# Low parts of eight mixed right sides at each layer border: GpSimd in place of VectorE

## The chip, the core and the metric

The kernel runs on one core of one Trainium2 chip. A core has five engines that run side by side and wait for each other by semaphores: TensorE (PE, matmuls; its weight loads are shown as PEld), VectorE (DVE), ScalarE (ACT), GpSimd (POOL), and SyncE (SP), which here only issues transfers. The metric is the device time of one execution in microseconds, lower is better.

## What is computed

Two transformer layers, one after the other, on a sequence of 1024 tokens with 1024 channels, all in float32:

```python
# first layer (one of depth 1), x: [1, 1024, 1024]
h = rmsnorm(x, norm1_g); proj = h @ w_in            # differential and forgetting attention
...
x = x + mix @ w_out
h2 = rmsnorm(x, norm2_g)
x = x + (silu(h2 @ w_gate) * (h2 @ w_up)) @ w_down
x = rmsnorm(x, normf_g)
# second layer
p = rmsnorm(x, g_attn_2) @ w_in_2                   # two convolutions, stick-breaking attention
...
x = x + concatenate([y_a, y_b, y_c]) @ w_out_2
h2 = rmsnorm(x, g_ffn_2)
x = x + square(relu(h2 @ w_ff1_2)) @ w_ff2_2
return rmsnorm(x, g_final_2)
```

In the kernel the norm's gain is applied ahead of the product and its root behind it, when the product leaves PSUM.

## The kernel before

**Products in three matmuls.** PE multiplies in a format that is shorter than float32. So each factor is a high part (a rounded copy, made by ScalarE) and a low part (the factor minus its high part). A product of one 128x128 block of weights with 128x512 columns is three matmuls: high by high (L1606), low weights by high (L1608), high weights by low (L1611). The low parts of the weights are made on GpSimd (L2408, `lows` or `late_r`, out of `values` or `late` and `wh`), their high parts on ScalarE (L2172). L1611 is the only one of the three that waits for the low part of the right side.

**Right sides.** They are the two big buffers R0 and R1, each with high and low parts of eight rows of 128x1024. The new input of a feed-forward part goes to R1: its row e is made when the output projection of the attention (`second_pass`) gives row e of X. VectorE adds up X (L1970, from PSUM), ScalarE rounds it to the high part (L2321) and VectorE makes the low part (L2026, 128x1024). PE mixes two works there: the last rows of the output projection and the first tiles of the next product (`dense_together`), which take row e of R1 as soon as it is there.

**The layer border.** So I call the stretch from the first L1970 to the first down product: 639 to about 720 us in the first layer, 1787 to about 1861 us in the second. (It lies between the attention and the feed-forward part of a layer.) The sum of the squares of X for the norm's root is taken there as well: ScalarE squares a row (L2331), GpSimd adds it to `mix` (L2467, 128x1024), PE sums over partitions (L1651), VectorE scales (L1821), ScalarE takes the root in two steps (L2215, L2219) and VectorE makes it exact (L1834 to L1838). With that root the first tiles leave PSUM (L2036, L2045 in the first layer, L2065 in the second), and their banks become free for other products.

**The mixed right sides.** Most feed-forward products are done in Strassen's way, seven products in place of eight (`dense_seven`; the products are called P1 to P7). Four of the seven take sums and differences of quarters of the input as their right side. They are made once at each border and kept in R0: for j = 0 to 3 and a = 0 to 3 the steps

- `right_z` (ScalarE, L2182), once for each j;
- `right_sum` (VectorE, L2002): X times gain, plus or minus another, 128x512, to R0f;
- `right_hi` (ScalarE, L2187): the high part;
- `right_lo` (VectorE, L2009): the low part, 128x512, sum minus high part.

P6, P5, P7 and P4 of the first group of seven read a = 1, 0, 2 and 3 in this order (the table `SEVEN_FIRST`, and `first_ready`, which says what each waits for). P7 and P4 are the last two; their eight low parts, a = 2 and a = 3, are the eight later ones.

**What sets the order.** Nobody writes it out. Each step says what it needs and gives; `engine_orders` lays the steps out by an estimate of their durations, gives each a due time from who needs it, and repeats that three times. It keeps the order among steps of one kind on one engine and chooses freely among kinds. So moving a step to another engine also moves its neighbours. PSUM has eight banks; a product waits until what stood in its bank has been taken out (`claim`, `next_bank`), for the down products by L2013, which adds PSUM to X.

## Time and profile before

| | us |
|---|---|
| three runs, median | 2492.11 |
| three runs, lowest and highest | 2489.48, 2495.3 |
| the profiled execution, device time | 2491.23 |
| its span in the profile | 2489.4 |
| busy in the span: PE, DVE, ACT, POOL | 2436.0, 1711.6, 1029.5, 1045.9 |

The span lies 1.8 us under the device time of the same execution. Times in the rows below count from the start of the span. A row of the timeline gives start and duration, the line of the kernel, the operation, what it writes and reads with shapes, how many neighbours of one kind are merged (x2), and in square brackets how long the engine had been idle before and who ended that. A record of DVE lasts until its last write; the next may start some 0.08 us before that.

### The profile page before, as it was taken

The page shows a single profiled execution, that of the slowest core. Times are in us where ns is not written, and L with a number is a line of the kernel's source. Part 1 is how long each engine was busy: PE and PEld are TensorE (multiplying, and loading weights), DVE is VectorE, ACT ScalarE, POOL GpSimd, SP SyncE. Part 2 cuts the span into 40 slices and gives each one's busy share as a digit, 9 for nine tenths or more (in the row PEclk, how much of TensorE's full clock was granted, in tenths as well). Part 3 has the DMA queues.
Part 4 walks back from the last instruction along what each step waited for, and adds up shares of the span by engine and source line. Part 5 has one row for each costly group of instructions (what it writes and reads, how often), then busy time and mean ns, then how long its engine had stood idle before and what let it go on. Part 6 is the DMA issues. An engine that isn't in the chain of part 4 may idle for free.

```text
span 2489.4 us, 31281 instructions
## 1 busy us (share of the span) xinstructions
PE 2436.0 (98%) x11654; PEld 1999.9 (80%) x11654; DVE 1711.6 (69%) x2373; ACT 1029.5 (41%) x1735; POOL 1045.9 (42%) x718
## 2 busy tenths in 40 slices
PE   9999999999899999999999999999989999999998
PEld 7776788888688888888887878887868888888886
DVE  6766757673786666666679866777497666666663
ACT  6455656552542322222246436554252232323233
POOL 4666552211534444444454553331343343434344
PEclk9999999999999999999999999999999999999998
DMA  4211221132111111111123852223211111112121
GB/s 162 76 56 47 86 60 44 54 116 76 39 47 53 55 55 56 51 51 51 55 59 111 188 127 68 60 76 105 66 39 56 47 56 47 57 46 60 43 64 72
DMA packets 156261, 170.20 MB, mean 68 GB/s; under 512 B 11088, under 2 KB 114256, under 8 KB 155984
## 3 DMA queue, kind: packets, MB, share of 16 engines
q1 hardware_dynamic: 152944, 156.67, 20.9%
q0 software_dynamic: 3168, 11.54, 2.5%
q8 instruction: 94, 1.54, 0.3%
q14 instruction: 55, 0.45, 0.1%
HBM read 122.55 MB, written 15.20 MB: 55 GB/s over the span
## 4 chain that ended last, share of the span: by engine, by line
PE 87%; DVE 6%; ACT 2%; issue 2%; POOL 1%; DMA 1%; SPq 0%; DVEq 0%; POOLq 0%; ACTq 0%
PE PS L1606 25%; PE PS L1611 25%; PE PS L1608 25%; PE PS L1702 3%; PE PS L1689 2%; PE PS L1723 2%; PE PS L1720 2%; PE PS L1683 2%; DVE R0f L2002 1%; DVE R L2026 1%; PE PS L1686 1%; DVE X L1970 1%; PE PS L1688 0%; DVE sm L1887 0%; PE PS L1670 0%
## 5 line engine op out<-in xcount | busy, mean ns | idle before, releaser
L1606 PE MATMUL PS<-R,wh 128*128 128x512 f32 x2952 | 1167.1, 395 | 3.9 <-DVE XP L1964 0.9
L1611 PE MATMUL PS<-R,wh 128*128 128x512 f32 x2952 | 1153.8, 391 | 14.3 <-DVE R L2026 14.1
L2408 POOL TENSOR_TENSOR lows<-values,wh 128x512 fp32r<-128x512 f32 (+1 forms) x410 | 596.0, 1456 | 1039.9 <-ACT wh L2172 931.8
L1608 PE MATMUL PS<-R,lows 128*128 128x512 f32 x2512 | 980.7, 390 | 1.6 <-POOL lows L2408 1.6
L1611 PEld LDWEIGHTS PS<-R,wh 128*128 128x128 f32 x2952 | 554.8, 188 | 137.6 <-DVE R L2026 19.2
L1606 PEld LDWEIGHTS PS<-R,wh 128*128 128x128 f32 x2952 | 555.7, 188 | 115.5 <-issue 4.1
L2172 ACT ACTIVATE wh<-values 128x512 fp32r<-128x512 f32 (+1 forms) x411 | 256.0, 623 | 721.4 <-PE PS L1611 685.0
L1608 PEld LDWEIGHTS PS<-R,lows 128*128 128x128 f32 x2512 | 472.7, 188 | 94.2 <-issue 4.1
L2013 DVE TENSOR_TENSOR X<-PS,X 128x512 f32<-128x512 f32 x400 | 272.2, 690 | 237.3 <-PE PS L1611 237.2
L2408 POOL TENSOR_TENSOR late_r<-late,wh 128x512 fp32r<-128x512 f32 x83 | 122.5, 1476 | 136.8 <-ACT wh L2172 97.5
L1608 PE MATMUL PS<-R,late_r 128*128 128x512 f32 x440 | 171.2, 389 | 0.0
L1990 DVE TENSOR_TENSOR stage<-PS,stage 128x512 f32<-128x512 f32 x154 | 104.5, 687 | 80.9 <-PE PS L1611 79.9
L2284 ACT ACTIVATE PT<-PS 128x512 fp32r<-128x512 f32 (+1 forms) x200 | 108.1, 552 | 101.2 <-PE PS L1702 94.0
L1689 PE MATMUL PS<-R 128*128 128x512 f32 (+2 forms) x288 | 116.8, 406 | 0.0
L1683 PE MATMUL PS<-R 128*128 128x512 f32 (+2 forms) x288 | 108.3, 376 | 6.5 <-ACT Pb L2267 4.0
L1887 DVE TENSOR_REDUCE sm<-PS 128x1 f32<-128x128 f32 (+7 forms) x128 | 95.5, 750 | 27.2 <-PE PS L1689 26.6
L1702 PE MATMUL PS<-ident,Pb 128*128 128x128 f32 x720 | 107.3, 274 | 5.1 <-DVE Pb L1899 3.2
L1911 DVE TENSOR_TENSOR_SCAN Pb<-TABF,vec 128x128 f32<-128x128 f32 (+3 forms) x64 | 97.1, 1521 | 17.5 <-ACT TABF L2276 9.1
L2172 ACT ACTIVATE wh<-late 128x512 fp32r<-128x512 f32 x83 | 52.3, 631 | 128.6 <-PE PS L1611 112.7
L1702 PEld LDWEIGHTS PS<-ident,Pb 128*128 128x128 f32 x720 | 85.9, 141 | 23.1 <-issue 6.4
L1934 DVE TENSOR_TENSOR PT<-PS,PT 128x512 fp32r<-128x512 f32 (+1 forms) x120 | 74.8, 631 | 33.4 <-ACT PT L2284 32.9
L1608 PEld LDWEIGHTS PS<-R,late_r 128*128 128x128 f32 x440 | 82.6, 188 | 17.1
(269 smaller groups left out, 2812.9 us busy)
## 6 DMA issues: line engine op xcount, KB each, us to landing
values<-w_in_dram SPq DMA_DIRECT2D x88, 256.0 KB, 2.9
values<-w_ff_dram SPq DMA_DIRECT2D x88, 256.0 KB, 2.8
R<-R SPq DMA_DIRECT2D x96, 128.0 KB, 2.3
X<-X POOLq DMA_DIRECT2D x22, 512.0 KB, 5.8
values<-w_up_dram SPq DMA_DIRECT2D x38, 256.0 KB, 3.0
values<-w_gate_dram SPq DMA_DIRECT2D x36, 256.0 KB, 2.9
late<-w_ff_dram SPq DMA_DIRECT2D x36, 256.0 KB, 2.9
values<-w_down_dram SPq DMA_DIRECT2D x32, 256.0 KB, 2.7
```

The source lines that it names most:

```text
L1606: e.matmul(PS[:, b, :], wh, high, start=s["start"], stop=False)
L1608: e.matmul(PS[:, b, :], wl, high, start=False, stop=False)
L1611: m = e.matmul(PS[:, b, :], wh, low, start=False, stop=s["stop"])
L1683: e.matmul(S2[:, k0:k1], q, u.KH[:, a, k0:k1], start=True, stop=False)
L1689: m = e.matmul(S2[:, k0:k1], q, u.KL[:, a, k0:k1], start=False, stop=True)
L1702: m = e.transpose(PS[:, s["tb"], at:at + 128], T.Pb[:, s["slot"], par, 128 * kt:128 * kt + 128], T.ident[:, :])
L1911: e.tensor_tensor_scan(dst[:, ::-1], bt[:, ::-1], T.zeros(n), 1.0, ALU.mult, ALU.add).then_inc(*sg.up("p", j["key"]))
L1990: e.tensor_tensor(stage[s["i"]], PS[:, s["b"], :], stage[s["k"]], ALU.add).then_inc(*sg.up("seven", s["key"]))
L2013: e.tensor_tensor(x, PS[:, s["b"], :], x, ALU.add).then_inc(*sg.up("x", s["key"]))
L2172: e.activation(T.wh[:, piece.h, 0:m], T.wv[piece.v][:, 0:m], ACT.Copy).then_inc(*sg.up("w_hi", piece.n))
L2284: e.activation(T.PT[:, s["x"], 0, 0:m], PS[:, s["tb"], 0:m], ACT.Copy, bias=bias).then_inc(*sg.up("pt_hi", key))
L2408: e.tensor_tensor(T.wl[piece.v][:, 0:m], T.wv[piece.v][:, 0:m], T.wh[:, piece.h, 0:m].bitcast(F), ALU.subtract).then_inc(*sg.up("w_lo", pi ...
```

## The change

The eight low parts with a = 2 and a = 3 are made by GpSimd, with the same subtraction, and counted on a semaphore of their own, `right_late_lo`. The products P7 and P4 of the first group wait for that one. Two waits of VectorE stay as they were for a = 0 and a = 1.

```diff
--- before.py
+++ after.py
@@ -1321,7 +1321,7 @@
 
     def first_ready(tag):
         rows = [[("post_hi", (tag, e)), ("post_lo", (tag, e))] for e in range(8)]
-        sums = [[[("right_hi", (tag, j, a)), ("right_lo", (tag, j, a))] for j in range(4)] for a in range(4)]
+        sums = [[[("right_hi", (tag, j, a)), ("right_lo" if a < 2 else "right_late_lo", (tag, j, a))] for j in range(4)] for a in range(4)]
         return dict(P1=rows[0::2], P2=rows[1::2], P3=rows[1::2], P5=sums[0], P6=sums[1], P7=sums[2], P4=sums[3])
 
     mix_ready = [[] for _ in range(8)]
@@ -2000,12 +2000,11 @@
             for before in {0: [], 1: [0], 2: [], 3: [0, 1, 2]}[a]:
                 w.wait_ge(*sg.at("right_sum", (tag, j, before)))
             e.scalar_tensor_tensor(out, x, g, other, ALU.mult, ALU.add if a == 1 else ALU.subtract).then_inc(*sg.up("right_sum", (tag, j, a)))
-        elif kind == "right_lo":
+        elif kind == "right_lo" and s["a"] < 2:
             j, a, tag = s["j"], s["a"], s["tag"]
             lo, hi = T.right(1, j, a), T.right(0, j, a)
             w.wait_ge(*sg.at("right_hi", (tag, j, a)))
-            if a < 2:
-                w.wait_ge(*sg.at("right_sum", (tag, j, (1, 3)[a])))
+            w.wait_ge(*sg.at("right_sum", (tag, j, (1, 3)[a])))
             e.tensor_tensor(lo, T.right_sum(j, a), hi.bitcast(F), ALU.subtract).then_inc(*sg.up("right_lo", (tag, j, a)))
         elif kind == "down_evac":
             x = T.XF[:, s["e"], cols(s["half"])]
@@ -2448,6 +2447,11 @@
             e.tensor_tensor(va, va, y, ALU.mult).then_inc(*sg.up("sub_part", (key, 3)))
             w.wait_ge(*sg.at("sub_part", (key, 3)))
             e.tensor_tensor(m, m, va, ALU.mult).then_inc(*sg.up("sub", key))
+        elif kind == "right_lo" and s["a"] > 1:
+            j, a, tag = s["j"], s["a"], s["tag"]
+            w.wait_ge(*sg.at("right_hi", (tag, j, a)))
+            e.tensor_tensor(T.right(1, j, a), T.right_sum(j, a), T.right(0, j, a).bitcast(F), ALU.subtract).then_inc(
+                *sg.up("right_late_lo", (tag, j, a)))
         elif kind == "tap_add":
             k, c = s["k"], s["chain"]
             w.wait_ge(*sg.at("tap_product", (c, k)))
```

On the engines, VectorE loses eight L2009 (L2008 in the changed kernel) at each border, GpSimd gains eight (L2453). Lines behind the first edit shift: L2009 becomes L2008, L2026 L2025, L2036 L2035, L2045 L2044, L2013 L2012, L2408 L2407 and L2467 L2471. PE keeps its instructions; the two L1651 stand two products later at each border. SyncE's order is unchanged.

On GpSimd at the first border, from the sum at 656.99 us, `mix` being the sum of squares. Before:

```order
L2467 TENSOR_TENSOR mix<-mix,P_61 128x1024 x2
L2408 TENSOR_TENSOR lows<-values,wh 128x512
L2467 TENSOR_TENSOR mix<-mix,P_61 128x1024
L2408 TENSOR_TENSOR lows<-values,wh 128x512
L2467 TENSOR_TENSOR mix<-mix,P_61 128x1024
L2408 TENSOR_TENSOR lows<-values,wh 128x512
L2467 TENSOR_TENSOR mix<-mix,P_61 128x1024
L2408 TENSOR_TENSOR lows<-values,wh 128x512 x2
```

In the changed kernel:

```order
L2471 TENSOR_TENSOR mix<-mix,P_61 128x1024
L2453 TENSOR_TENSOR R_49<-R0f,R_49 128x512
L2471 TENSOR_TENSOR mix<-mix,P_61 128x1024
L2407 TENSOR_TENSOR lows<-values,wh 128x512
L2471 TENSOR_TENSOR mix<-mix,P_61 128x1024
L2453 TENSOR_TENSOR R_49<-R0f,R_49 128x512
L2471 TENSOR_TENSOR mix<-mix,P_61 128x1024
L2407 TENSOR_TENSOR lows<-values,wh 128x512 x2
L2471 TENSOR_TENSOR mix<-mix,P_61 128x1024
L2453 TENSOR_TENSOR R_49<-R0f,R_49 128x512
L2407 TENSOR_TENSOR lows<-values,wh 128x512
L2453 TENSOR_TENSOR R_49<-R0f,R_49 128x512 x3
```

Two of the new subtractions (L2453) stand between the sums of squares, one weight subtraction has slipped from ahead of the sum of row 6 to behind it, and four more follow the last sum. The last two stand behind five and six more weight subtractions; at the second border, which else reads alike, behind two and three.

On VectorE at the first border, from the two L2002 at 673.13 us, over the eighth L2026 to the scaling of the row sums (L1821). Before:

```order
L2002 SCALAR_TENSOR_TENSOR R0f<-X,vec,R0f 128x512 x2
L2026 SCALAR_TENSOR_TENSOR R_50<-X,vec,R_50 128x1024
L2009 TENSOR_TENSOR R_49<-R0f,R_49 128x512
L2002 SCALAR_TENSOR_TENSOR R0f<-X,vec,R0f 128x512
L2009 TENSOR_TENSOR R_49<-R0f,R_49 128x512
L2002 SCALAR_TENSOR_TENSOR R0f<-X,vec,R0f 128x512
L1821 TENSOR_SCALAR stage<-PS 128x512 x2
```

In the changed kernel:

```order
L2002 SCALAR_TENSOR_TENSOR R0f<-X,vec,R0f 128x512 x2
L2025 SCALAR_TENSOR_TENSOR R_50<-X,vec,R_50 128x1024
L2002 SCALAR_TENSOR_TENSOR R0f<-X,vec,R0f 128x512 x2
L2008 TENSOR_TENSOR R_49<-R0f,R_49 128x512
L2002 SCALAR_TENSOR_TENSOR R0f<-X,vec,R0f 128x512 x2
L1821 TENSOR_SCALAR stage<-PS 128x512 x2
```

Up to the eighth L2026 (L2025) the order is the same. Behind it stand four single instructions of DVE ahead of L1821 before, five now, with one low part among them instead of two. Further on, all eight low parts that are left to VectorE stand ahead of the first L2012, and with them one L1990 and one L2035; before, four L2013 stood ahead of that L1990 and eight ahead of that L2036. At the second border eight L2008 and nine L2002 stand between the eighth L2025 and the first L2012, before eleven L2009 and eight L2002.

## Rows read from the trace of the kernel before

**Rows 1.** part 1 of the page: busy us (share of span) xinstructions

```profile
PE 2436.0 (98%) x11654; PEld 1999.9 (80%) x11654; DVE 1711.6 (69%) x2373; ACT 1029.5 (41%) x1735; POOL 1045.9 (42%) x718
```

**Rows 2.** waits of PE, 636 to 760 and 1790 to 1900: us, times, longest

```profile
PE PS L1611 <- DVE R L2026: 7.1, 6, 2.5
...
PE PS L1611 <- DVE R L2026: 7.0, 6, 2.5
```

**Rows 3.** timeline of PE, first border: start, duration, line, operation, tiles, idle before

```profile
677.76 0.50 PE L1611 MATMUL PS<-R,wh 128*128 128x512 f32 x1 [2.51 <-DVE R L2026]
...
683.53 0.39 PE L1606 MATMUL PS<-R,wh 128*128 128x512 f32 x1
```

**Rows 4.** busy time by stretch: length, engines PE to POOL, PEclk, DMA

```profile
677.60:718.70 41.10, 40.94 (x170) 32.62 (x171) 39.43 (x52) 22.10 (x34) 14.63 (x9) 0.96 0.15 45
...
678.60:682.10 3.50, 3.50 (x8) 1.95 (x7) 3.50 (x4) 0.63 (x1) 1.35 (x1) 0.51 0.00 0
```

**Rows 5.** DVE by group, 639 to 677.5: count, busy us, mean ns, idle

```profile
L2002 DVE SCALAR_TENSOR_TENSOR R0f<-X,vec,R0f 128x512 f32<-128x512 f32 x7 | 16.0, 2303 | 0.0
...
L1970 DVE TENSOR_TENSOR X<-PS,XP 128x512 f32<-128x512 f32 x16 | 10.5, 680 | 0.0
```

**Rows 6.** timeline of POOL, first border

```profile
637.39 1.29 POOL L2408 TENSOR_TENSOR lows<-values,wh 128x512 fp32r<-128x512 f32 x1 [6.67 <-ACT wh L2172]
...
661.64 2.40 POOL L2467 TENSOR_TENSOR mix<-mix,P 128x1024 f32<-128x1024 f32 x1 [2.24 <-ACT P L2331]
...
676.51 3.44 POOL L2467 TENSOR_TENSOR mix<-mix,P 128x1024 f32<-128x1024 f32 x1 [0.55 <-ACT P L2331]
```

**Rows 7.** timeline of DVE, first border

```profile
660.48 1.27 DVE L2026 SCALAR_TENSOR_TENSOR R<-X,vec,R 128x1024 fp32r<-128x1024 f32 x1
...
662.27 2.32 DVE L2002 SCALAR_TENSOR_TENSOR R0f<-X,vec,R0f 128x512 f32<-128x512 f32 x1
...
671.93 1.28 DVE L1970 TENSOR_TENSOR X<-PS,XP 128x512 f32<-128x512 f32 x2
...
676.43 1.27 DVE L2026 SCALAR_TENSOR_TENSOR R<-X,vec,R 128x1024 fp32r<-128x1024 f32 x1
...
677.63 2.87 DVE L2009 TENSOR_TENSOR R<-R0f,R 128x512 fp32r<-128x512 f32 x1
...
718.70 1.87 DVE L2013 TENSOR_TENSOR X<-PS,X 128x512 f32<-128x512 f32 x3
```

**Rows 8.** POOL by group, 680 to 718.6

```profile
L2408 POOL TENSOR_TENSOR lows<-values,wh 128x512 fp32r<-128x512 f32 x6 | 9.2, 1534 | 22.5 <-ACT wh L2172 12.4 <-DVE values L1984 10.1
L2408 POOL TENSOR_TENSOR late_r<-late,wh 128x512 fp32r<-128x512 f32 x2 | 3.1, 1560 | 2.3 <-ACT wh L2172 2.3
```

**Rows 9.** timeline of ScalarE, first border

```profile
659.99 0.63 ACT L2187 ACTIVATE R<-R0f 128x512 fp32r<-128x512 f32 x1 [1.42 <-DVE R0f L2002]
```

**Rows 10.** DVE by group, 677.6 to 718.6

```profile
L2009 DVE TENSOR_TENSOR R<-R0f,R 128x512 fp32r<-128x512 f32 x13 | 13.3, 1026 | 0.0
...
L2002 DVE SCALAR_TENSOR_TENSOR R0f<-X,vec,R0f 128x512 f32<-128x512 f32 x9 | 9.3, 1035 | 0.0
...
L2050 DVE TENSOR_TENSOR stage<-stage 128x512 f32<-128x512 f32 x2 | 2.4, 1230 | 0.0
```

**Rows 11.** DVE by group, 1825.7 to 1859.3

```profile
L2002 DVE SCALAR_TENSOR_TENSOR R0f<-X,vec,R0f 128x512 f32<-128x512 f32 x8 | 10.7, 1338 | 0.0
L2009 DVE TENSOR_TENSOR R<-R0f,R 128x512 fp32r<-128x512 f32 x11 | 9.5, 874 | 0.0
```

**Rows 12.** POOL by group, 1828.1 to 1859.3

```profile
L2408 POOL TENSOR_TENSOR lows<-values,wh 128x512 fp32r<-128x512 f32 x4 | 7.7, 1919 | 19.4 <-ACT wh L2172 19.4
L2408 POOL TENSOR_TENSOR late_r<-late,wh 128x512 fp32r<-128x512 f32 x1 | 1.3, 1297 | 1.8 <-ACT wh L2172 1.8
```

**Rows 13.** timeline of DVE, second border

```profile
1825.77 3.46 DVE L2009 TENSOR_TENSOR R<-R0f,R 128x512 fp32r<-128x512 f32 x2
```

**Rows 14.** timeline of PE, second border

```profile
1860.08 0.50 PE L1606 MATMUL PS<-R,wh 128*128 128x512 f32 x1 [0.59 <-DVE X L2013]
```

## The prediction

> **What bounds the kernel now.** I read part 1 of the page first: TensorE (PE) is busy for 2436.0 us of a 2489.4 us span [rows 1], so an edit on VectorE (DVE) or GpSimd (POOL) counts only where PE waits for one of them or would begin to. The waits of PE around the first layer border come next: 7.1 us in six waits, all for L2026, the low part of a row of the new input that DVE makes [rows 2]. The second border has the same six, 7.0 us. After the last of the six PE resumes at 677.76 [rows 3] and hardly waits again: in 677.6 to 718.7 it is busy for 40.94 of 41.10 us. DVE, though, is busy for 39.43 of the same 41.10 us [rows 4]. Between a border's last L2026 and its first L2013 (the sums that empty PE's banks after the first down product) DVE is nearly full, and the moved instructions lie there.
>
> **How DVE and POOL meet.** The third thing to see is a mutual block. An L2002 whose inputs both lie in SBUF takes 2303 ns on average in 639 to 677.5 us, while L1970, whose first input lies in PSUM, keeps 680 ns through the same POOL work [rows 5]. Single rows show the shape of it. POOL's sum at 661.64 runs 2.40 us to 664.04; DVE's L2002 issued at 662.27 takes 2.32 us, to 664.59, and has about 0.7 us of its own work, so it started at about 663.9, some 0.15 us before POOL's end [rows 6, 7]. Undisturbed, POOL needs 1.29 us for a 128x512 subtraction and 2.40 for a 128x1024 sum [rows 6]. So whoever asks first goes first, and a DVE instruction with two SBUF inputs that comes behind a POOL subtraction loses up to 1.29 - 0.15 = 1.14 us. The Trainium skill, "SBUF — State Buffer", section "Who interferes with whom", states such a rule: DVE with two SBUF inputs and a GpSimd instruction that reads SBUF block each other fully, for the whole instruction, by order of issue. The trace agrees but for the 0.15 us; with the whole 1.29 us as the price of a meeting the sum below would grow by about 2 us. It speaks against this change.
>
> **What the change removes and adds.** Each border has 16 low parts; eight leave DVE. As seconds on DVE each is worth 0.60 us of issue (an undisturbed 678 ns record overlaps the next by about 0.08). On POOL each is a subtraction of two SBUF tiles of the same shape as L2408, 1.29 us. The same L2002, L2187 and matmuls stay, the transfers keep their order, and PE's order changes only in that the two row sums (L1651) stand two products of three matmuls later (6 x 0.227 = 1.36 us). No added wait stands on PE's way by itself: its products with the mixed sides come more than 15 us after the low parts are ready, by my count of the matmuls between. On POOL the new waits for right_hi stand ahead of weight subtractions (L2408); POOL is idle for 22.5 us before those in 680 to 718.6 [rows 8], and that hides the waits, though not the port.
>
> **Step 1, up to the eighth L2026.** DVE's order is unchanged here; POOL's has two more instructions, one before the sum at 661.64, one in place of a weight subtraction, which slips behind. Replayed with the rule above, in us:
> - The first moved subtraction is ready at 659.99 + 0.63 = 660.62 [rows 9]. DVE's L2026 holds the port from 660.48 to 661.67 [rows 7]; POOL runs 661.67 to 662.96.
> - DVE's L2002 then goes at 662.8 instead of 663.9, a gain of 1.1. But the POOL sum ready since 661.6 now runs 663.5 to 665.9 instead of from 661.64 [rows 6], and the next L2026, after two free L1970, waits for it: it ends at 666.9 as before. The gain is gone.
> - The weight subtraction to 668.2, L2002 to 668.7, sum to 671.1, L2026 to 672.15 (before: L1970 starts at 671.93 [rows 7], so 0.2 late).
> - The second moved subtraction 672.15 to 673.45, L2002 to 674.0, sum to 676.4, L2002 to 676.9, weight subtraction to 678.2, and the eighth L2026 from 678.05 to 679.25. Before it was issued at 676.43 and the next one started at 677.63, so it is 1.6 us late.
> In the kernel before, this L2026 was issued 0.08 us ahead of the last POOL sum, at 676.51 [rows 6, 7], and so did not wait. Bounds: a gain of 2 us, were the early 1.1 kept twice; a loss of 2.4, were it to fall behind a whole sum. I take +1.6, the replay, with the rows themselves as its terms.
>
> **Step 2, from the eighth L2026 to the first L2013.** First border, DVE's own work: 13 L2009 become 8, minus 5 x 0.60 = -3.0; one L1990 and one L2036 now stand ahead of the L2013 that stood behind, +1.2; together -1.8. POOL's work: six of the moved subtractions and the slipped weight subtraction come in, seven. What does one cost DVE? Rows by group show it: 13 L2009 at 1026 ns (13 x 0.348 = 4.5 over 678), nine L2002 at 1035 (undisturbed 0.74: 2.7), two L2050 at 1230 (1.1), 8.3 us in all [rows 10]. The last sum of squares took 2.2 of them (the L2009 at 677.63 lasts 2.87 us instead of 0.68 [rows 7]), the eight weight subtractions [rows 8] 6.1, that is 0.76 each. Seven at 0.76: +5.3. With step 1: 1.6 - 1.8 + 5.3 = +5.1 us. If each meets a waiting DVE: 7 x 1.14 = 8.0, so +7.8.
> Second border: 11 L2009 become 8 and an L2002 comes ahead, -1.8 + 0.7 = -1.1. Eight L2002 at 1338 ns (4.8) and 11 L2009 at 874 (2.2) lost 7.0 [rows 11], of which the last sum took 2.2 (two L2009 in 3.46 us instead of 1.28 [rows 13]), five weight subtractions [rows 12] 4.8: 0.96 each. Seven: +6.7. With step 1: +7.2; at most +8.5.
>
> **Step 3, does PE feel it?** Border 1: L2013 starts at 718.70 and its first instruction lasts 0.68 us, to 719.38 [rows 7]. The matmuls that take this bank stand 53 products behind the one that starts at 683.53 [rows 3], at 0.681 us each 719.6. The slack is 0.2 us, so it hides nothing worth counting. Border 2: PE waited 0.59 us for exactly this L2013, at 1860.08 [rows 14]: no slack. The gate and up evacuations (L2036, L2045) lie in the same queue and would show part of the delay first, as PE waits at about 705 to 712 us; that is the same delay, not another. PE is bound everywhere else, so nothing is won back later.
>
> **Sum.** +5.1 + 7.2 = +12.3 us. The profiled execution took 2491.23 us, 0.9 below the median of 2492.11; 2491.23 + 12.3 = 2503.5, and I say 2503.
>
> **Rivals.**
> - Cover holds (no change within 0.2%). The moved subtractions fall under DVE instructions that read PSUM (L2036, L2045, L1821, L2013) or into DVE's idle time, and cost nothing; step 1 comes out at 0 to +1.6. For it: the weight subtraction at 637.39 met nobody [rows 6]. Against it: DVE has only 41.10 - 39.43 = 1.7 us free [rows 4], and by its order only ten of its 52 instructions there read PSUM. Then DVE is 1.8 and 1.1 shorter, PE does not speed up, and the time is 2491 to 2494. Chance 0.16.
> - Faster. The one mechanism: in the critical stretch the early 1.1 us of step 1 is kept, because the short subtraction breaks up the meetings with the long sums; it decides if the eighth L2026 ends before 677.6. At most 2 us a border, and with the last PE wait under its 2.5 us [rows 2] the half clock behind it could go too. That clock: in 678.6 to 682.1 the granted clock was 0.51 [rows 4], the 1.2 GHz level, right after PE's 2.5 us of idleness, a loss of about 1.7 us. Both borders: -2 x 3.7 = -7.4, 2484. Against it: the sum that is pushed back meets the very next L2026. Chance 0.07.
> - Slower still. The new PE waits (I expect some of 2 to 3 us at 705 to 720) each bring such a half clock of 1.7 us, and DVE meets POOL nearly every time: 7.8 + 8.5 + 2 x 1.7 = +19.7, 2511. Chance 0.19.
> - The move is carried out as the text says, by the orders above, so that it doesn't do what it says has no chance of its own; that POOL reaches a right side too late for PE would need over 15 us and gets 0.01, within slower.
>
> **Chances and range.** The forecast has 0.57, the slower cases 0.20, no change 0.16, faster 0.07. A measurement of this kernel can tell about 0.2%, 5 us, from no change, so up to 2497 counts as the same. Faster 0.07, same 0.16, slower 0.77. Eight in ten: from 2492, inside the no-change case, to 2512, the top of the sum with its half clocks. Inside the likeliest case alone it is 2499 to 2508.
>
> **What would show it.** Right: the profile after has, at both borders, PE waits between the eighth L2025 (L2026 before) and the first down sums for the evacuations at L2035, L2044 or L2012 that were not there, 2 to 6 us in sum; L2002 with a mean well over 1035 ns in that stretch; the last L2471 sum ending 2 to 4 us later; the eighth L2025 some 1 to 2 us later. Wrong: PE busy through that stretch as before (step 3), moved subtractions beside DVE rows of 0.68 us (the price of a meeting), or the eighth L2025 earlier than 677.6 (step 1). If the PE waits at the six low parts shrink under 7.1 us, the rival on the other side is the one.

## The result: 0.37% slower, and the profile after

The changed kernel takes 2502.32 us (median of six runs, 2501.02 to 2503.36), the kernel before 2492.75 beside it (six runs, 2488.33 to 2495.89). The ratio is 1.0037, 95% interval 1.0027 to 1.0047. A second comparison, below, gave 1.0054, 1.0041 to 1.0068. The forecast was 2503, slower. Three runs of the experiments below (one of e1, two of e3) took 3460 to 3462 us at a mean granted clock of 0.65; medians and ratios leave them out.

The profiled execution of after took 2501.84 us, its span is 2499.9. The line that answers to [rows 1] shows little change in how much the engines have to do. GpSimd is busy 26 us longer, VectorE 2 us longer although it has 16 instructions less, TensorE (PE) the same:

```profile
PE 2436.2 (97%) x11654; PEld 1999.7 (80%) x11654; DVE 1713.8 (69%) x2357; ACT 1028.4 (41%) x1735; POOL 1071.8 (43%) x734
```

(One execution is profiled, so single stretches are compared from a common mark: the first L1970 of a border, at 639.34 and 1787.48 us before, 637.36 and 1791.80 after.)

**Where PE lost it.** These are the waits of PE at the first border of after (in total, times, longest), as in [rows 2]:

```profile
PE PS L1611 <- DVE R L2025: 8.1, 6, 3.7
PE PS L1606 <- DVE X L2012: 2.0, 1, 2.0
PE PS L1606 <- DVE mix L2044: 2.0, 1, 2.0
```

and at the second:

```profile
PE PS L1611 <- DVE R L2025: 7.7, 6, 3.3
PE PS L1606 <- DVE X L2012: 2.7, 1, 2.7
PE PS L1611 <- DVE R L2068: 1.0, 1, 1.0
```

The six waits for the low parts of the new input grew from 7.1 and 7.0 to 8.1 and 7.7 us, and behind them stand new ones, for VectorE's evacuations (L2044), its down sums (L2012) and a low part of the layer's hidden tile (L2068): 4.0 us at the first border, 3.7 at the second (0.6 before, [rows 14]). (A wait of 0.8 us for L1990 at the first border is in both kernels.) The busy time of PE in the 47 us behind the mark and in the 73 us behind those (length, busy, granted clock, DMA share, GB/s) gives the whole account. Before:

```profile
639.34:686.34 47.00, 39.93 (x158) 0.96 0.13 41
686.34:759.34 73.00, 72.22 (x319) 1.00 0.16 47
1787.48:1834.48 47.00, 39.95 (x159) 0.96 0.15 45
1834.48:1907.48 73.00, 72.41 (x320) 1.00 0.15 44
```

After:

```profile
637.36:684.36 47.00, 38.94 (x149) 0.93 0.12 40
684.36:757.36 73.00, 68.23 (x298) 1.00 0.15 44
1791.80:1838.80 47.00, 39.29 (x150) 0.93 0.14 43
1838.80:1911.80 73.00, 69.19 (x303) 1.00 0.14 42
```

Idle time goes from 7.1 + 0.8 + 7.0 + 0.6 = 15.5 to 8.1 + 4.8 + 7.7 + 3.8 = 24.4 us. The granted clock of the 47 us falls from 0.96 to 0.93 at the first border and 0.94 at the second. Added up over stretches of 4 us, as (1 - granted clock) x length, the two borders lost 3.4 us to it before and 6.8 after. I call idle time plus lost clock of these 240 us the **border loss**: 18.9 us before, 31.2 after, +12.3.

The lost clock comes in portions of 1.7 us. Each is a stretch of 3.4 us at 1.2 in place of 2.4 GHz that begins soon after a PE wait. After has two at each border; the first border's are these:

```profile
671.80:675.20 3.40, 2.34 (x6) 1.34 (x4) 3.40 (x2) 1.75 (x3) 3.40 (x3) 0.57 0.00 0
678.60:682.10 3.50, 3.50 (x11) 2.77 (x10) 3.50 (x2) 0.68 (x2) 3.09 (x2) 0.58 0.00 0
```

The first follows a wait of 2.0 us that ended at 669.86, the second the wait of 3.67 us that ended at 677.81. Before has only one, behind the 2.51 us of [rows 3].

Lost clock differs from run to run as well. Taken as (1 - mean granted clock) x span and averaged over all runs, it is 24.0 us in the second comparison (e9) against 16.9 for the kernel before beside it, so up to half of the 14 us there is lowered clock.

**Where VectorE (DVE) and GpSimd (POOL) meet.** This is VectorE by group (count, busy us, mean ns) between the eighth L2025 and the first L2012, the stretches that answer to [rows 10, 11]:

```profile
L2002 DVE SCALAR_TENSOR_TENSOR R0f<-X,vec,R0f 128x512 f32<-128x512 f32 x9 | 12.9, 1454 | 0.0
L2008 DVE TENSOR_TENSOR R<-R0f,R 128x512 fp32r<-128x512 f32 x8 | 9.1, 1153 | 0.0
```

```profile
L2002 DVE SCALAR_TENSOR_TENSOR R0f<-X,vec,R0f 128x512 f32<-128x512 f32 x9 | 13.4, 1513 | 0.0
L2008 DVE TENSOR_TENSOR R<-R0f,R 128x512 fp32r<-128x512 f32 x8 | 6.8, 875 | 0.0
```

L2002 went from 1035 to 1454 ns at the first border, from 1338 to 1513 at the second. Single meetings can be read by holding two timelines side by side. GpSimd's:

```profile
658.69 2.21 POOL L2453 TENSOR_TENSOR R<-R0f,R 128x512 fp32r<-128x512 f32 x1 [1.29 <-ACT R L2186]
...
692.47 1.48 POOL L2453 TENSOR_TENSOR R<-R0f,R 128x512 fp32r<-128x512 f32 x1 [4.16 <-ACT R L2186]
```

and VectorE's:

```profile
675.47 2.29 DVE L2025 SCALAR_TENSOR_TENSOR R<-X,vec,R 128x1024 fp32r<-128x1024 f32 x1
677.68 4.56 DVE L2002 SCALAR_TENSOR_TENSOR R0f<-X,vec,R0f 128x512 f32<-128x512 f32 x2
...
692.84 1.66 DVE L1838 SCALAR_TENSOR_TENSOR rstd<-stage 128x512 f32<-128x512 f32 x1
...
723.33 1.87 DVE L2012 TENSOR_TENSOR X<-PS,X 128x512 f32<-128x512 f32 x3
```

L2453 is the moved subtraction. Undisturbed a 128x512 subtraction takes GpSimd 1.29 us; the one at 692.47 lasts 1.48, to 693.95. L1838, two inputs in SBUF, was issued at 692.84 and lasts 1.66 us, to 694.50, with 0.69 of its own: it started at 693.81, 0.14 us before GpSimd's record ends, and lost 0.97. The one at 658.69 shows the other direction: VectorE's L2025 (658.48 to 659.75) held it up, and it lasts 2.21 us.

### The profile page after: what moved, and what is told of

It reads as the page before. It is cut to its first block, busy times and chain, and to the rows that moved or that the text cites. A ratio compares the mean times of both kernels' runs of the same rounds, so it can differ in the third digit from the quotient of the medians.

```text
span 2499.9 us, 31279 instructions
## 1 busy us (share of the span) xinstructions
PE 2436.2 (97%) x11654; PEld 1999.7 (80%) x11654; DVE 1713.8 (69%) x2357; ACT 1028.4 (41%) x1735; POOL 1071.8 (43%) x734
## 4 chain that ended last, share of the span: by engine, by line
PE 84%; DVE 8%; issue 2%; ACT 2%; POOL 2%; DMA 2%; SPq 0%; DVEq 0%; POOLq 0%; ACTq 0%
PE PS L1606 24%; PE PS L1608 23%; PE PS L1611 23%; PE PS L1702 3%; PE PS L1689 2%; PE PS L1723 2%; DVE R0f L2002 2%; PE PS L1720 2%; PE PS L1683 2%; DMA X<-X 1%; DVE R L2025 1%; PE PS L1686 1%; DVE X L1970 1%; DVE sm L1887 0%; PE PS L1688 0%
## 5 line engine op out<-in xcount | busy, mean ns | idle before, releaser
L2407 POOL TENSOR_TENSOR lows<-values,wh 128x512 fp32r<-128x512 f32 (+1 forms) x410 | 594.8, 1453 | 1017.6 <-ACT wh L2171 914.9
L2012 DVE TENSOR_TENSOR X<-PS,X 128x512 f32<-128x512 f32 x400 | 272.7, 690 | 249.3 <-PE PS L1611 249.3
L2407 POOL TENSOR_TENSOR late_r<-late,wh 128x512 fp32r<-128x512 f32 x83 | 123.4, 1487 | 132.4 <-ACT wh L2171 93.2
L1990 DVE TENSOR_TENSOR stage<-PS,stage 128x512 f32<-128x512 f32 x154 | 104.5, 687 | 79.6 <-PE PS L1611 78.6
```

Of the source, the lines that this page charges most:

```text
L1990: e.tensor_tensor(stage[s["i"]], PS[:, s["b"], :], stage[s["k"]], ALU.add).then_inc(*sg.up("seven", s["key"]))
L2012: e.tensor_tensor(x, PS[:, s["b"], :], x, ALU.add).then_inc(*sg.up("x", s["key"]))
L2407: e.tensor_tensor(T.wl[piece.v][:, 0:m], T.wv[piece.v][:, 0:m], T.wh[:, piece.h, 0:m].bitcast(F), ALU.subtract).then_inc(*sg.up("w_lo", pi ...
```

## Experiments

All times of one group were taken on one chip beside the kernel before (median 2493.83 for the first four, 2493.59 for the next four, 2492.05 for e9 to e11, 2493.46 for e12). In this table the marks are us from a border's first L1970, first border / second border: to the start of the instruction behind the eighth L2025 (L2026), and to the first L2012 (L2013). Border loss is defined above; it comes from one profiled execution each, the ratio from all runs.

| kernel | median us | ratio to before, 95% | behind eighth low part | first down sum | border loss (idle + clock) |
|---|---|---|---|---|---|
| before | | 1 | 38.29 / 38.29 | 79.36 / 71.87 | 18.9 (15.5 + 3.4) |
| after | 2502.32 | 1.0037 [1.0027, 1.0047] | 40.32 / 40.31 | 85.97 / 77.72 | 31.2 (24.4 + 6.8) |
| e1 one fill | 2493.77 | 1.0005 [0.9994, 1.0015] | 38.27 / 38.27 | 78.18 / 71.25 | 18.4 (15.0 + 3.4) |
| e2 order of before | 2492.20 | 0.9995 [0.9987, 1.0004] | 38.26 / 38.28 | 79.39 / 71.88 | 18.1 (14.7 + 3.4) |
| e3 late | 2489.68 | 0.9984 [0.9975, 0.9994] | 38.26 / 38.28 | 77.69 / 68.55 | 17.3 (13.9 + 3.4) |
| e4 on ScalarE | 2495.66 | 1.0005 [0.9997, 1.0014] | 38.86 / 38.87 | 78.98 / 70.07 | 21.6 (14.8 + 6.8) |
| e5 two held | 2504.51 | 1.0040 [1.0026, 1.0054] | 38.28 / 38.29 | 84.93 / 76.84 | 28.1 (21.3 + 6.8) |
| e6 three fills | 2495.76 | 1.0003 [0.9995, 1.0012] | 39.30 / 39.28 | 80.26 / 71.54 | 23.9 (17.1 + 6.8) |
| e7 only a = 3 | 2499.45 | 1.0021 [1.0012, 1.0030] | 39.37 / 39.36 | 81.49 / 75.45 | 25.4 (20.3 + 5.1) |
| e8 only j = 0 | 2498.83 | 1.0017 [1.0008, 1.0026] | 40.33 / 40.34 | 80.96 / 72.07 | 25.8 (19.0 + 6.8) |
| e9 after again | 2505.88 | 1.0054 [1.0041, 1.0068] | 40.31 / 40.35 | 85.92 / 76.61 | 32.5 (24.0 + 8.5) |
| e10 late again | 2489.99 | 0.9993 [0.9985, 1.0002] | 38.27 / 38.26 | 76.70 / 68.54 | 16.1 (12.7 + 3.4) |
| e11 late, sums held | 2484.14 | 0.9963 [0.9949, 0.9977] | 32.55 / 32.55 | 72.39 / 65.34 | 8.8 (8.8 + 0) |
| e12 sums held | 2488.97 | 0.9983 [0.9975, 0.9992] | 32.54 / 32.56 | 76.26 / 66.11 | 16.4 (11.3 + 5.1) |

**The port, or the new orders?** In e1 each moved step keeps its place in the orders of after, but fills its target with zeros and reads nothing, so these low parts are left out of the result.

```diff
-            e.tensor_tensor(T.right(1, j, a), T.right_sum(j, a), T.right(0, j, a).bitcast(F), ALU.subtract).then_inc(
-                *sg.up("right_late_lo", (tag, j, a)))
+            e.memset(T.right(1, j, a).bitcast(F), 0.0).then_inc(*sg.up("right_late_lo", (tag, j, a)))
```

> The changed kernel with the eight moved subtractions of each border replaced by GpSimd instructions that only write (zeros into the same 128x512 place, so these eight low parts are left out of the result). The orders of all engines are those of the changed kernel. Port theory (a GpSimd instruction that reads SBUF holds up VectorE's with two SBUF inputs): no meeting with these writes, the border's way from first L1970 to first L2012 shrinks from 86.0 back to 79 us or less, time 2489 to 2494 us. Rival, order theory (the planner's new order of VectorE and GpSimd costs by itself, through waits for ScalarE and for GpSimd's queue): the time stays near 2502.

The cost was gone: 1.0005, and the marks are those of before or earlier. The orders alone cost nothing: those of VectorE, ScalarE and PE are the ones of after, instruction by instruction. The fill on GpSimd and, issued 0.2 us before it, an L2025 of VectorE with two SBUF inputs run side by side, each at its undisturbed length:

```profile
662.58 0.52 POOL L2453 MEMSET R<- 128x512 f32 x1 [1.28 <-ACT R L2186]
```

```profile
662.38 1.27 DVE L2025 SCALAR_TENSOR_TENSOR R<-X,vec,R 128x1024 fp32r<-128x1024 f32 x1
```

But the fill took 0.52 us where the subtraction takes 1.29. So time in GpSimd's queue was still a suspect. e6 makes three fills of each step, one after the other, 1.69 us in all, in the same orders.

```diff
-            e.tensor_tensor(T.right(1, j, a), T.right_sum(j, a), T.right(0, j, a).bitcast(F), ALU.subtract).then_inc(
-                *sg.up("right_late_lo", (tag, j, a)))
+            for key in ((tag, j, a, 1), (tag, j, a, 2), (tag, j, a))[0 if PLANNED else 2:]:
+                e.memset(T.right(1, j, a).bitcast(F), 0.0).then_inc(*sg.up("right_late_lo", key))
+                if len(key) == 4:
+                    w.wait_ge(*sg.at("right_late_lo", key))
```

> The write-only test with the time filled up: each of the eight moved subtractions of a border is three write-only fills of its 128x512 target, one after the other, on GpSimd, with the engine orders of the kernel after; the eight low parts are left out of the computation. One fill took 0.52 us in the run before this, less than the 1.29 of the subtraction, so that run left open whether the port or the time in GpSimd's queue is what costs. Three take about 1.6 us, more than the subtraction. Port theory (only reading two tiles from SBUF blocks VectorE): as with one fill, 2492 to 2495 us. Queue theory (GpSimd's sums and weight subtractions, and with them VectorE and TensorE, come late because GpSimd is occupied): at least the 2502 of the kernel after.

1.0003, with an upper end of 1.0012, below the 1.0027 at which the interval of after begins. Behind the eighth L2025 nothing of the delay is left: 80.26 - 39.30 = 40.96 us to the first L2012, against 41.07 before and 45.65 after. VectorE keeps its undisturbed length beside the three fills, whichever comes first. An L2025 issued 0.19 us before them takes 1.27 us, and an L2008 that starts 0.50 us before the end of a third fill takes 0.68:

```profile
660.96 1.69 POOL L2454 MEMSET R<- 128x512 f32 x3 [1.27 <-ACT R L2186]
...
681.19 1.69 POOL L2454 MEMSET R<- 128x512 f32 x3
```

```profile
660.77 1.27 DVE L2025 SCALAR_TENSOR_TENSOR R<-X,vec,R 128x1024 fp32r<-128x1024 f32 x1
...
682.38 0.68 DVE L2008 TENSOR_TENSOR R<-R0f,R 128x512 fp32r<-128x512 f32 x1
```

Ahead of the eighth L2025, though, e6 has half of the delay of after (39.30 us; 38.29 before, 40.32 after). There the filled-up queue pushes the sums of squares back, and these do read. So reads from SBUF on both engines explain all of Step 2 and at least half of Step 1. At most the other half of Step 1 is the time in GpSimd's queue, and rather less, since three fills take 1.69 us and the subtraction 1.29. The border loss of this profile would cost 5.0 us; the runs show at most 3.

The rule that the prediction drew on (the Trainium skill, "SBUF — State Buffer", "Who interferes with whom") says also that a VectorE instruction with two SBUF inputs does not contend with a GpSimd instruction that only writes. These traces agree: 1.27 us beside a fill of 0.52.

**Place or number?** e2 moves the same eight subtractions, but after the orders have been laid out as for the kernel before: each goes to GpSimd at the time at which VectorE's plan had it, behind the eighth L2026 of its border, and VectorE's other steps keep their order.

```diff
...
+        if engine == "vector" and part.step["kind"] == "right_lo" and part.step["a"] > 1:
+            engine = "gpsimd"
+        rows[engine].append((part.start, len(rows[engine]), part.step))
+    rows["gpsimd"].sort(key=lambda row: row[:2])
...
```

> The same eight subtractions of each border on GpSimd, but all engines keep the order that the kernel before has: VectorE's with eight taken out, GpSimd's with eight put in where VectorE had them, all behind the eighth L2026. Step 1 of the prediction can't cost anything then. If seven extra GpSimd subtractions at 0.76 to 0.96 us of lost VectorE time each are the whole price wherever they stand (price theory): step 2 alone, 5.3 - 8 x 0.6 = +0.5 us at the first border and about +2 at the second, 2495 us. Rival, that the count of moved instructions alone decides: 2502 as the changed kernel. Second rival, step 1 and what stands ahead of the row sums make nearly all of the 10 us: 2492 to 2494.

No cost: 0.9995, and the marks of before. 2492.20 is under the 2495 of the price theory and in the range of the second rival, and the marks of after fit that rival too. From the instruction behind the eighth low part to the end of the row sums' scaling (the second L1821), after takes 9.80 and 9.72 us at the two borders, before 6.10 and 5.92. From there to the first down sum it is 35.85 and 27.70 against 34.97 and 27.66: the meetings there are about covered by the work that was saved. In e2 only one moved subtraction of each border runs ahead of that scaling, in after three.

Seven L2009 lie between the eighth L2026 and the first L2013 where before had thirteen, and one L2002 more: 6 x 0.60 - 0.66 = 2.9 us of VectorE's own work gone, against 1.8 in after. Six moved subtractions run before 720.4 us, as many as in after. The way between the two marks is that of before, so they cost some 2.9 us together, 0.5 each. So the number alone does not set the price. The new orders of after, which alone cost nothing in e1, put the moved steps early.

e3 takes after and lets each moved subtraction wait for the fourth of the first down sums.

```diff
             w.wait_ge(*sg.at("right_hi", (tag, j, a)))
+            w.wait_ge(*sg.at("x", (tag, 0, 1, 1)))
```

> The changed kernel with one more wait: GpSimd makes the eight low parts only after the fourth down sum (L2012), where VectorE reads PSUM most of the time and P7 and P4 are still some 20 us away. Port theory with place: no meetings in the full stretch, VectorE freed of eight subtractions there; the border's way is 77 to 79 us, and the time 2489 to 2492, at or a little below the kernel before. Rival (GpSimd is too slow for them wherever they stand, or PE waits for the low parts at P7): 2497 or more, with PE waits for L2454.

0.9984, faster than before and after. (The wait is known to the planner, which lays out all engines anew, so this run changes the neighbours' order along with the place.) GpSimd makes the first of the eight at 723.15 us, 4 us behind the first L2012 of 719.15, and VectorE's low parts at the second border are undisturbed:

```profile
L2008 DVE TENSOR_TENSOR R<-R0f,R 128x512 fp32r<-128x512 f32 x8 | 5.3, 677 | 0.0
```

The repetition, e10, gave 0.9993 [0.9985, 1.0002], so that a gain is small, 1 to 4 us, and not proved. The two runs are one kernel and differ in lost clock: on average e3 lost 15.2 us against 18.4 for the kernel before beside it, e10 16.7 against 16.9. Part of e3's gain is therefore chance.

> The kernel with the eight moved low parts held back on GpSimd behind the fourth first down sum, once more, to settle whether it is faster than the kernel before. Theory (the moved work now meets VectorE only where TensorE doesn't wait for it): ratio 0.998 to 0.999 again, 2489 to 2492 us. Rival (the first result was chance): 1.000 within 0.05%.

e4 gives the eight to ScalarE, as plain copies of the sums (the high part is not subtracted).

```diff
...
+        elif kind == "right_lo" and s["a"] > 1:
+            j, a, tag = s["j"], s["a"], s["tag"]
+            w.wait_ge(*sg.at("right_hi", (tag, j, a)))
+            e.activation(T.right(1, j, a), T.right_sum(j, a), ACT.Copy).then_inc(*sg.up("right_late_lo", (tag, j, a)))
...
```

> The eight low parts are given to ScalarE as plain copies of the sums (so they are not the low parts, and the result is off), on ScalarE's own way to SBUF. VectorE gets the same relief as in the changed kernel and GpSimd none of the load. Port theory: time at or just below the kernel before, 2489 to 2493. Rival, that the new plan that comes with VectorE's relief costs by itself: 2497 to 2502.

1.0005: no cost that can be told, and no gain, although VectorE is rid of 4.8 us a border and its L2008 are undisturbed (678 ns, eight of them, in 675 to 716.1 us). ScalarE's copies delay the eighth L2025 by 0.6 us, and PE's time at a lowered clock grows: the profile has a second portion at each border (6.8 us in all), and over all runs the lost clock is 22.4 us against 18.4. That takes up what VectorE saves behind the eighth.

**How much is Step 1, how much Step 2?** e5 is after with the two moved subtractions of j = 0 put behind the last sum of squares in GpSimd's order.

```diff
...
+    held, rest = [step for step in pool if early(step)], [step for step in pool if not early(step)]
...
+    for step in rest:
+        orders["gpsimd"].append(step)
+        if step["kind"] == "post_square" and step.get("e") == 7 and step.get("half") is None:
+            orders["gpsimd"] += [low for low in held if low["tag"] == step["name"]]
```

> The kernel after, complete computation, with one move in GpSimd's order: at each border the two moved subtractions of j = 0, which stand among the sums of squares, go behind the last sum. VectorE's and TensorE's orders stay those of the kernel after. It separates the two stretches. Theory (a meeting costs VectorE time wherever it falls): the +2.0 us at the eighth L2025 of each border goes (its distance from the border's first L1970 is 38.3 us again, not 40.3), but the two meetings fall behind it, where one cost 0.75 to 0.96 us, so +1.7 a border comes back: 2 x (-2.0 + 1.7) = -0.6, 2499 to 2503 us, ratio to the kernel before about 1.0035. Rival one (only the critical stretch counts, meetings behind it fall into slack): -4.0 and nothing back, 2498. Rival two (GpSimd's queue before the eighth L2025 was not the cause): 40.3 us stays and the time too, 2502.

The 2.0 us at the eighth went at both borders (38.28), and 1.0 and 1.1 us came back behind it (84.93 - 38.28 = 46.65 against 45.65; 38.55 against 37.41), 0.5 a meeting where I had written 0.75 to 0.96. The time, 2504.51 or 1.0040, is no better than that of after, although the border loss of the profile is 3.1 us smaller; the interval of the ratio is too wide to tell. At the first border the wait moved to the evacuations, where one of 2.3 us now brings a lowered clock:

```profile
PE PS L1611 <- DVE R L2025: 7.1, 6, 3.5
PE PS L1606 <- DVE mix L2044: 2.7, 2, 2.3
```

e8 is the counterpart: only those two move, the six others stay on VectorE.

```diff
-        elif kind == "right_lo" and s["a"] > 1:
+        elif kind == "right_lo" and s["a"] > 1 and s["j"] == 0:
...
```

> A quarter of the change, complete computation: only the two low parts with j = 0, a = 2 and a = 3 of each border on GpSimd, the two that in the kernel after stand among the sums of squares ahead of the eighth L2025; the orders are planned again. Theory: those two delay the eighth L2025 by 2.0 us at each border (40.3 us from the first L1970 instead of 38.3), VectorE has two subtractions less behind it (-1.2): 2 x (2.0 - 1.2) = +1.6 to +4, 2494 to 2497 us. Rival (they meet nobody or win, only the six others cost): 2490 to 2493 us and 38.3 us or less.

40.33 us at both borders, as in after, and 1.0017, 4 us. Its first down sums come only 1.6 and 0.2 us later than before, PE does not wait for them, and yet it pays, because PE waits at the eighth L2026 itself (this is either border):

```profile
PE PS L1611 <- DVE R L2026: 9.1, 6, 4.8
```

The 1.2 us that VectorE saves behind the eighth are worth nothing here. Lowered clock behind this longer wait is a large part of the cost: over all runs the lost clock is 23.6 us against 20.0. e7 moves the four with a = 3 only.

```diff
-        elif kind == "right_lo" and s["a"] > 1:
+        elif kind == "right_lo" and s["a"] == 3:
...
```

> Half of the change, complete computation: only the four low parts with a = 3 of each border on GpSimd, those with a = 2 stay on VectorE; the orders are planned again. Price times count: half of the border sum of +12.5 us, with or without the 2 us that was won ahead of the border, 2497 to 2499 us. Rival (the first few meetings cost nothing because VectorE has 1.7 us of idle time, and only the full eight overrun it): 2493 to 2495. Rival two (what costs is that low parts stand in the critical stretch at all, whatever their number): 2500 to 2502.

1.0021, about half of the cost for half of the steps. The first rival (nothing until all eight are moved) falls; the 2500 us of the second lie just inside the interval. One of the four stands ahead of the eighth (39.37 us), and at the second border PE waits for the down sum again:

```profile
PE PS L1606 <- DVE X L2013: 2.7, 1, 2.7
```

**What the rest of the execution does.** e9 is the changed kernel once more.

> The kernel after once more, beside the kernel before on the same chip. In its first profile the 120 us behind the first L1970 of the two borders held 12.3 us more of PE idleness and lost clock than before, but the rest of the execution lost 3 to 4 us less to lowered clock than the kernel before (none at all in the stretches near 540, 1370 and 1570 us where before loses it). If that gift belongs to the kernel (other phases at the same waits), it is there again: rest at 8 us of lost clock, ratio 1.0037 or less. If it was the chance of one execution, the rest loses 12 to 16 us as in the others, and the ratio is 1.004 to 1.005.

The border loss is 32.5 us and the ratio 1.0054. Outside the borders this execution lost 17.0 us to lowered clock, the first profile of after 8.1, the one of before 12.8. The profiled execution of after lost the least of its six runs (14.9 us of clock in all, their mean is 19.6), so what was missing in that profile was chance. A wait shows how: both profiles of after have one of 2.02 us ahead of the first down product. In the first the clock behind it stayed up, in e9 it fell:

```profile
724.40:727.80 3.40, 3.40 (x16) 1.00 0.00 0
```

```profile
726.40:729.80 3.40, 3.40 (x11) 0.70 0.00 0
729.80:733.00 3.20, 3.20 (x13) 0.79 0.00 0
```

**A version that beats both.** In [rows 5] seven L2002 at 2303 ns stand in the stretch where PE waits. e11 is the late kernel in which the sums of j = 0, 1 and 2 wait for the eighth L2025, as those of j = 3 do.

```diff
-        x = [("post_hi", (tag, 2 * j + 1)), ("post_lo", (tag, 2 * j + 1))]
+        x = [("post_hi", (tag, 2 * j + 1)), ("post_lo", (tag, 7 if j < 3 else 2 * j + 1))]
```

> Complete computation. The late kernel, and in addition the sums L2002 of j = 0, 1 and 2 wait for the eighth low part L2025 as those of j = 3 do, so that VectorE has only L1970 and L2025 in the critical stretch. In the kernel before, seven L2002 stand there at 2303 ns each. Theory (VectorE's sums in the critical stretch, in their meetings with GpSimd's sums of squares, delay the low parts that TensorE waits for): the six waits of TensorE fall from 7.1 us a border to 3 or less and the lowered clock behind them (1.7) may go; 4 to 5 us a border less, and VectorE has then up to 5 us more to do behind the eighth L2025, of which the held low parts gave back 4.8: 2483 to 2488 us. Rival (GpSimd's sums alone delay each L2025, whatever VectorE does between): the six waits stay over 5 us and the sums that are now late bring waits at the first down products, 2492 to 2500 us.

2484.14 us, 0.9963 [0.9949, 0.9977], 18 to 22 us below the changed kernel. The six waits of 7.1 us became two of 1.6, and no clock is lost in the 47 us behind the mark. The first border:

```profile
PE PS L1611 <- DVE R L2025: 1.6, 2, 1.4
```

```profile
639.78:686.78 47.00, 44.72 (x190) 1.00 0.15 45
686.78:759.78 73.00, 72.02 (x315) 1.00 0.16 47
```

e12 has the sums held and the moved subtractions not (after plus the line above).

> Complete computation. The kernel after with the sums L2002 held as in the run before (those of j = 0, 1 and 2 wait for the eighth L2025), but the moved low parts not held: GpSimd makes them as soon as they are ready. Against the run before it differs in the place of the eight moved low parts alone. Theory (early low parts meet VectorE between the eighth L2025 and the first down products, and TensorE waits there): the six waits stay at 1.6 us a border, and waits at the evacuations and first down products come, 3 to 5 us a border: 2490 to 2495 us. Rival (with the critical stretch cleared VectorE has idle time enough, and the place no longer matters): 2483 to 2486 us as in the run before.

0.9983, some 5 us more than e11, though the two intervals just touch (0.9975 and 0.9977). The six waits are as short, and the waits at the down sums are back, with lowered clock behind them (5.1 us at the two borders):

```profile
PE PS L1606 <- DVE X L2012: 3.5, 1, 3.5
```

So the place of the moved subtractions costs also where the critical stretch is clear, though less (7.6 us of border loss instead of 31.2 - 17.3 = 13.9). This is likely and not shown cleanly, since the wait that e11 has and e12 has not also changes VectorE's and ScalarE's orders. The sums held with all low parts on VectorE, the version that would show what e11 owes to GpSimd, was not run.

## Why the prediction was right, step by step

- **Step 1** (+1.6 us a border). Measured +2.0 at both, from the marks. The mechanism was right: the eighth L2025, issued before at 37.09 us from the mark and free, now waits for GpSimd (2.29 us for 1.27). But the replay had one weight subtraction between the last two sums of squares where the order has two, the one that slipped and its neighbour (L2407 x2 at 673.28 us, ahead of the last sum at 676.64). The replay also left out the effect on PE. This delay goes to PE's longest wait and, in e8 and after, comes with a second portion of 1.7 us of lowered clock at each border. e8 shows that PE pays it even where VectorE later catches up.
- **Step 2.** First border +3.5 expected (5.3 - 1.8), +4.6 measured (45.65 - 41.07); second +5.6 expected, +3.8 measured (37.41 - 33.58). The count of seven was wrong. The slipped weight subtraction runs ahead of the last sum, in Step 1's stretch; behind the eighth stand eight weight subtractions at the first border and five at the second, as many as before, and six moved ones come in. One of those cost (4.6 + 1.8) / 6 = 1.06 us at the first border, not 0.76, and (3.8 + 1.1) / 6 = 0.82 at the second, not 0.96. Against e1, which has the orders of after and no reads, the way behind the eighth is 5.7 and 4.4 us longer (45.65 - 39.91, 37.41 - 32.98), 0.96 and 0.74 for each of the six. With six at the prediction's own prices the forecast would have been +10.6 us, 2502. The mechanism, reads of two tiles from SBUF on both engines, was right (e1, e6). The prices were off in opposite directions and the count was too high, and the sum is good partly for that reason; this much is luck. A mean price taken from other steps carried only to 15 to 40%, since the order of the meetings decides.
- **Step 3** (PE has no slack). Right: the first L2012 came 6.6 and 5.8 us later, and the border loss grew by 12.3 us in all, against +12.3 forecast. Its form was other than I wrote, 8.9 us of idle time and 3.4 of lowered clock. I had put lowered clocks into the rival alone, at nothing in the sum, and the delay of VectorE (6.6 and 5.8 us) at its full length into PE's idle time. Idle time came out smaller and the clock made up for it: luck again. In the second comparison it did not balance as well (+13.8).
- **The sum.** 2503.5 forecast; 2502.32 and 2505.88 measured, +9.6 and +13.8 to the medians beside them. The account of one execution closes only to some 3 us, since the clock outside the borders varies by as much and some matmul records are missing.
- **The rivals.** Cover: it does not hold for after, but e2 and e3 show that it can be had by another place. Faster: the six waits would have had to shrink; they grew to 8.1 and 7.7. Slower still: its extra portions of lowered clock came (one a border, two at the first in e9). Its price of 1.14 us for every meeting was nearly reached at the first border (1.06) and not at the second (0.82).
- **What would show it.** PE waits of 2 to 6 us between the eighth low part and the first down sums: 4.0 and 3.7. L2002 well over 1035 ns at the first border: 1454. The last sum of squares 2 to 4 us later: by 2.0 from the mark (it ends at 679.95 and 679.99 us, and the mark of after lies 1.98 earlier). The eighth L2025 1 to 2 us later: issued 1.0, done 2.0 us later.

## What to carry to other kernels

Work that is taken from VectorE and given to GpSimd is not gone for VectorE if it reads SBUF: a 128x512 subtraction cost VectorE at most 1.1 us and on average 0.5 to 1.1, against the 0.60 saved. What decides is where it lies. The same eight steps cost 9 to 14 us as soon as they are ready, nothing among the steps they stood among before, and nothing or a little less once they wait until PE has its next inputs. And look first at what VectorE does while PE waits for it: moving the sums out of that stretch, one line, took 6 us off the late kernel (2489.99 to 2484.14) and more than 10 off the changed one, while no place of the low parts gave more than 4.

## What was unexpected of the hardware

- An instruction of VectorE that waited for GpSimd starts some 0.15 us before GpSimd's record ends (0.14 at 693.81 us of after).
- A 128x512 fill on GpSimd takes 0.52 us, less than half of a subtraction, and in e1 and e6 no VectorE instruction that had only fills beside it was held up.
- Lowered clock comes in portions of 1.7 us behind PE waits, and a wait of the same length is followed by it in one execution and not in another: 2.02 us, with a granted clock of 1.00 behind it in after and 0.70 and 0.79 in e9. Whether a change pays for it can't be read from one profile. Within one kernel it makes most of the scatter: over the 33 runs of before beside e1 to e4, a run with 1 us more lost clock took 0.7 us longer (correlation 0.85).
